# A three-block fp32 transformer kernel: how four norms are summed and awaited on TensorE, and how modulation slabs are scaled

## What is computed

```python
def rms_norm(x, gain):
    y = x * lax.rsqrt(jnp.mean(x * x, axis=-1, keepdims=True) + NORM_EPS)
    return y * gain
def modulate(x, shift, scale):
    return x * (1 + scale[:, None, :]) + shift[:, None, :]
def swiglu(u, w_in, w_out):
    gate, up = jnp.split(u @ w_in, 2, axis=-1)
    return (jax.nn.silu(gate) * up) @ w_out
# first block, for each layer
mod = c_act @ mod_w[layer] + mod_b[layer]
sh1, sc1, g1, sh2, sc2, g2 = jnp.split(mod, N_MOD, axis=-1)
u = modulate(rms_norm(h, norm_mix[layer]), sh1, sc1)
h = h + g1[:, None, :] * mix
u = modulate(rms_norm(h, norm_ffn[layer]), sh2, sc2)
h = h + g2[:, None, :] * swiglu(u, ffn_w_in[layer], ffn_w_out[layer])
# between the layers: shared keys and values from their own norm and modulation
# second block
x = x + rms_norm_2(mixed @ w_out, norm_mix_post)      # the norm "post2"
```

## Time and profile before

| | us |
|---|---|
| median of 3 runs (lowest, highest) | 2295.59 (2285.57, 2300.39) |
| the profiled execution: time | 2293.14 |
| the profiled execution: span, first to last instruction | 2291.3 |
| PE busy | 2157.5 (94% of the span) |
| DVE busy | 1407.9 (61%) |
| ACT busy | 748.5 (33%) |
| POOL busy | 443.2 (19%) |

### The profile page before, as it was taken

How to read it: one execution, slowest core, us unless ns; L and a number is a source line. 1 busy time by engine, 2 the same in 40 slices (tenths; PEclk the granted TensorE clock), 3 DMA queues, 4 the chain that set the end, 5 groups by cost and what they waited for, 6 DMA issues and landing times.

```text
span 2291.3 us, 25604 instructions
## 1 busy us (share of the span) xinstructions
PE 2157.5 (94%) x10020; PEld 1722.6 (75%) x10020; DVE 1407.9 (61%) x1943; ACT 748.5 (33%) x963; POOL 443.2 (19%) x283
## 2 busy tenths in 40 slices
PE   6999999889999989999899999998999998999997
PEld 3787887677888867756678888876568876888885
DVE  7866765556677674377354454477556766655656
ACT  4433243322222223356332222245224234222221
POOL 3000000089988953010000000000410100000000
PEclk9999999999999998999999999999999998999998
DMA  6642321235555543221123222322013221322220
GB/s 216 209 159 93 109 94 56 74 131 208 178 189 178 181 147 129 83 101 56 56 74 109 93 93 94 108 96 68 24 56 111 92 76 72 99 97 99 93 92 37
DMA packets 39371, 248.00 MB, mean 108 GB/s; under 512 B 4927, under 2 KB 5055, under 8 KB 11348
## 3 DMA queue, kind: packets, MB, share of 16 engines
q1 hardware_dynamic: 32820, 228.91, 29.0%
q0 software_dynamic: 3088, 11.16, 1.5%
q10 hardware_dynamic: 3344, 6.29, 0.8%
HBM read 240.05 MB, written 6.29 MB: 108 GB/s over the span
## 4 chain that ended last, share of the span: by engine, by line
PE 82%; DVE 7%; issue 5%; POOL 3%; ACT 2%; DMA 1%; SPq 0%; DVEq 0%; ACTq 0%; POOLq 0%
PE bank L714 24%; PE bank L716 23%; PE bank L715 23%; PE bank L975 2%; DVE w_lo L1934 2%; PE bank L1093 1%; ACT w_hi L1441 1%; PE bank L1103 1%; PE bank L1114 1%; POOL raw L603 1%; DVE scr L1969 1%; PE bank L748 1%; DMA pool<-in_filt_w 1%; PE bank L864 1%; POOL raw L604 1%
## 5 line engine op out<-in xcount | busy, mean ns | idle before, releaser
L714 PE MATMUL bank<-u_hi,w_hi 128*128 128x512 f32 x1708 | 693.7, 406 | 38.7 <-DVE w_lo L1934 11.7
L715 PE MATMUL bank<-u_lo,w_hi 128*128 128x512 f32 x1708 | 671.2, 393 | 0.0
L716 PE MATMUL bank<-u_hi,w_lo 128*128 128x512 f32 x1708 | 671.1, 393 | 0.0
L1934 DVE TENSOR_TENSOR w_lo<-raw,w_hi 128x2048 fp32r<-128x2048 f32 x160 | 424.6, 2654 | 219.6 <-ACT w_hi L1441 219.5
L714 PEld LDWEIGHTS bank<-u_hi,w_hi 128*128 128x128 f32 x1708 | 324.5, 190 | 128.6 <-issue 48.0
L1441 ACT ACTIVATE w_hi<-raw 128x2048 fp32r<-128x2048 f32 x160 | 305.3, 1908 | 346.0 <-PE bank L716 302.9
L716 PEld LDWEIGHTS bank<-u_hi,w_lo 128*128 128x128 f32 x1708 | 324.1, 190 | 69.7
L715 PEld LDWEIGHTS bank<-u_lo,w_hi 128*128 128x128 f32 x1708 | 325.0, 190 | 66.4 <-issue 3.8
L714 PE MATMUL bank<-g_hi,w_hi 128*128 128x512 f32 x772 | 306.6, 397 | 13.4 <-DVE w_lo L1934 6.4
L716 PE MATMUL bank<-g_hi,w_lo 128*128 128x512 f32 x772 | 301.9, 391 | 0.0
L715 PE MATMUL bank<-g_lo,w_hi 128*128 128x512 f32 x772 | 301.9, 391 | 0.0
(11 more groups left out here) (293 smaller groups left out, 2229.9 us busy)
## 6 DMA issues: line engine op xcount, KB each, us to landing
raw<-in_wts SPq DMA_DIRECT2D x216, 1024.0 KB, 4.8
spectra<-pool ACTq DMA_DIRECT2D x16, 256.0 KB, 2.0
scr<-in_rel POOLq DMA_DIRECT2D x16, 256.0 KB, 3.1
pool<-spectra POOLq DMA_DIRECT2D x16, 256.0 KB, 3.1
H<-in_x ACTq DMA_DIRECT2D x1, 2048.0 KB, 24.1
out<-H SPq DMA_DIRECT2D x8, 256.0 KB, 2.0
pool<-in_filt_w POOLq DMA_DIRECT2D x2, 512.0 KB, 12.0
pool<-in_window POOLq DMA_DIRECT2D x1, 1024.0 KB, 17.5
```

The lines of the kernel that those rows point to most:

```text
L714: pe.matmul(out, lh, rh, start=start, stop=False, skip_group_check=True)
L715: pe.matmul(out, lh, rl, start=False, stop=False, skip_group_check=True)
L716: return pe.matmul(out, ll, rh, start=False, stop=stop, skip_group_check=True)
L1934: dve.tensor_tensor(w_lo[RING[w]][:, :], raw[W_STREAM[w] % raw_ring][:, :], w_hi[RING[w]][:, :].bitcast(F32), ALU.subtract).then_inc(lo_do ...
```

## The change

Four things are changed, in the norms "ffn0", "kv", "ffn1" and "post2" and around them.

1. DVE adds only the squares of chunks 0 to 5. PE sums three tiles instead of one (`ssum`, the square of chunk 6 and the square of chunk 7, the last in a buffer of its own, `sq_last`). The add of the sixth square stands behind the last residual. The Sqrt table is loaded ahead of the squares (`root_table`).
2. Between and behind these sums PE repeats a product of two constants, 128x128, into the bank that the next slab will overwrite: 4, 3, 5 and 6 times (`busy`).
3. The slab behind each of these norms, and the first query slab and the gate slab `mgate`, take the two products with `u_hi` as soon as `u_hi` is there, and the product with `u_lo` two chunks later (one later for `mgate` and the first slab of the last stage).
4. The 36 modulation slabs leave the `raw` ring. POOL loads them by its own queue into three buffers `m_buf`, ACT multiplies them by the condition in 8 instructions of 128x256 right behind a weight copy, and POOL keeps the three sums.

```diff
+RING_ITEMS = []
+_m = 0
+for _s in STREAM:
+    _m += _s[0] == "M"
+    if _s[0] == "W" or _m <= M_POOLED:
+        RING_ITEMS.append(_s)
...
+SHORT = ("ffn0", "kv", "ffn1", "post2")
+ADDS = {name: 6 if name in SHORT else KC for name in MAIN}
+ADDED = {name: sum(ADDS[x] for x in MAIN if MAIN[x] < MAIN[name]) for name in MAIN}
...
+        m_buf = [pool[:, a:a + SLOT] for a in (4096, 6144, 12288)]
...
+            def load_mod(m):
+                i = m - M_POOLED
+                pl.dma_start(m_buf[i % 3], A["wts"][M_SOURCE + m]).then_inc(mod_in[i % 3], 16)
...
             def sum_mods():
+                pl.wait_ge(product, READY[FIRST["wo0"]])
+                for m in range(M_POOLED, M_POOLED + 3):
+                    load_mod(m)
                 pl.wait_ge(u_l, U_FFN0 + KC)
                 for m in range(M_POOLED, NM):
...
-                    link(pl.tensor_tensor(chunks, chunks, cact[:, :].unsqueeze(2).broadcast_to((P, KC, 256)), ALU.mult))
+                    pl.wait_ge(m_scaled, KC * (i + 1))
...
+                    if m + 3 < NM:
+                        pl.wait_ge(m_pooled, i + 1)
+                        load_mod(m + 3)
...
-            def norm(name):
+            def norm(name, target=None):
                 n = NORM[name]
...
+                pe.wait_ge(sq_add, ADDED[name] + ADDS[name])
+                pe.wait_ge(*released(n - 1))
+                for x, src in enumerate((ssum, sq[0], sq_last)):
+                    if x:
+                        pe.wait_ge(sq_done, 8 * MAIN[name] + 6 + x)
+                    for j in range(TB):
+                        mm = pe.matmul(bank[6][:, j:j + 1], src[:, j * P:(j + 1) * P], onec[:, :], start=(x == 0 and j == 0),
+                                       stop=(x == 2 and j == TB - 1), skip_group_check=True)
+                    if target is not None and x < 2:
+                        busy(target, (4, 3)[x])
+                mm.then_inc(n_col, 1)
+                if target is not None:
+                    busy(target, 5)
                 norm_bc(n)
+                if target is not None:
+                    busy(target, 6)
+
+            def busy(n, count):
+                b = claim(n)
+                for _ in range(count):
+                    pe.matmul(b[:, 0:P], ident[:, :], ones[:, :], start=True, stop=True)
+
+            def slot_lag(label, i, first, count, lag, nout=2):
+                w, hi, lo = weights(label, i)
+                banks = [claim(first + j) for j in range(nout)]
+                for k in range(KC + lag):
+                    if k < KC:
+                        pe.wait_ge(u_h, count + k + 1)
+                        for j in range(nout):
+                            c = k * 256 + j * P
+                            pe.matmul(banks[j][:, :], hi[:, c:c + P], u_hi[:, k, :], start=(k == 0), stop=False, skip_group_check=True)
+                            pe.matmul(banks[j][:, :], lo[:, c:c + P], u_hi[:, k, :], start=False, stop=False, skip_group_check=True)
+                    if k >= lag:
+                        x = k - lag
+                        wait_u(count + x + 1)
...
-            norm("post2")
-            lead = mlp_slot(0)
+            norm("post2", FIRST["mi0"])
+            lead = mlp_lead()
             follow = mlp_slot(1)
-            for k in range(KC):
+            for k in range(KC + 1):
                 next(lead)
                 if k >= 2:
                     next(follow)
...
+            def scale_mod(m):
+                i = m - M_POOLED
+                act.wait_ge(mod_in[i % 3], 16 * (i // 3 + 1))
+                for k in range(KC):
+                    x = m_buf[i % 3][:, k * 256:(k + 1) * 256]
+                    act.activation(x, x, ACT.Identity, bias=zcol[:, 0:1], scale=cact[:, k:k + 1]).then_inc(m_scaled, 1)
...
                     act.activation(w_hi[RING[w]][:, :], raw[s % raw_ring][:, :], ACT.Copy).then_inc(hi_done, 1)
+                    for m in range(M_POOLED, NM):
+                        if M_BEFORE[m] == w:
+                            scale_mod(m)
...
-            ffn("0", G_FFN0, 0, G2_0, "wo0", lambda c: add_square("kv", c))
-
-            add_square("kv", KC - 1)
+            ffn("0", G_FFN0, 0, G2_0, "wo0", lambda c: c < ADDS["kv"] and add_square("kv", c))
```

More of the change, by code:

```diff
@@ L453, in build @@
         rel_ready, mask_ready, taps_in = sem("rel_ready"), sem("mask_ready"), sem("taps_in")
+        m_scaled = sem("m_scaled")
+        mod_in = [sem(f"mod_in{x}") for x in range(3)]
         w4_in, row_done, row_out = sem("w4_in"), sem("row_done"), sem("row_out")
@@ L560, in _ @@
             w = m = 0
[L561 removed]
+            for s, item in enumerate(RING_ITEMS):
                 if s >= raw_ring:
@@ L1116, in weighted @@
                 mm.then_inc(at_v, 1)
-            for step in query_steps(0):
-                pass
+            slot_lag("qq", 0, FIRST["qq"], U_MIX1, 2)
             pe.wait_ge(mod_col, NVMOD)
@@ L1151, in _ @@
                 pass
-            norm("ffn1")
+            norm("ffn1", FIRST["fi1_0"])
             ffn("1", U_FFN1, G_FFN1)
@@ L1624, in _ @@
                 ahead("wo0", i)
+                if i == 0:
+                    root_table("ffn0")
                 squares("ffn0", H, (2 * i, 2 * i + 1))
```

100 lines of the change are left out of this document (68 added, 32 removed).

## The result

| kernel | median of runs, us | ratio to before, 95% interval |
|---|---|---|
| before | 2294.35 (7 runs, 2285.57 to 2301.25) | |
| changed | 2280.63 (7 runs, 2276.60 to 2283.89) | 0.9937 [0.9917, 0.9958] |

The changed kernel is 0.6% faster, 14.5 us by the ratio; 2281 us had been predicted. The profiled execution took 2281.22 us, with a span of 2279.4 us. The total was right and its terms were not: the modulation slabs gave far more than was put down for them, and the norms cost time where they were to win some.

The account below looks back on a forecast made before the run. PE, busy 94% of the span, bounds the kernel, with waits and half-clock products at norms. Terms -0.5 - 6.3 + 1.3 + 4.5 - 1.6 - 10 = -12.6 us gave 2280.5 profiled, 2281 us forecast; range 2263 to 2299.

Parts of the forecast that it names:

- The modulation slabs: First feed-forward stage: waits for split slabs and residuals (7.6 and 4.7 us) mostly vanish; -10 us, between 0 and -13.
- a return of the waits: First feed-forward stage: PE's waits might come back from ACT, whose scaling was put at 3.3 us per slab; gain then 0.
- a sum of -5 us: Whole kernel: if three splits on PE's path wait for POOL's sums, the slabs give -2 and the total is -5.
- ffn0: Norm "ffn0": second slab 2.9 us sooner if the clock holds, 1.8 us later if it falls; -0.5 us taken.
- kv: Norm "kv": collision of POOL with DVE's add goes, sums start earlier; -6.3 us, middle of -8.7 and -3.9.
- ffn1: Norm "ffn1": second slab 1.1 us sooner with the clock held or 3.7 us later with it fallen; +1.3 us taken.
- The prediction's own sign: Norms: the forecast fails if they gain more than 20 us or lose in sum, or if PE comes to wait for ACT.
- post2: Norm "post2": later root moves DVE's queue and the pair ends later, so the output slab starts 3.2 to 5.8 later; +4.5 us.
- First query slab: First query slab: starts some 0.9 us sooner on `u_hi`, may spare a clock fall; -1.6 us, between -2.6 and 0.
- The clock falls in all four: Rival, four norms: 18 extra products run at half speed, norms win nothing; -3.6 us, 2290 us, chance 0.22.
- The clock holds: Rival, four norms: constant products bridge them and keep full clock; -25.1 us, 2268 us, chance 0.24.
- The loads come late: Rival, modulation loads on POOL's queue: landing beyond about 22 us slows the kernel; some +25 us, 2318 us, chance 0.08.

Follow-up runs that it names:

- e1: Kernel before with only the modulation slabs changed: out of the ring, ACT scaling, POOL summing; norms and slab order untouched. 2269.15 us, ratio 0.9892.
- e5: Kernel before with the modulation slabs out of the ring, in buffers on POOL's queue, but POOL keeping its product. 2296.38 us, ratio 1.0016.
- e9: Changed kernel with its constant products moved from between the sums to ahead of the wait for them, more behind the broadcast. 2267.45 us, ratio 0.9889.
- e10: e8 with fifteen constant products ahead of the sums at "kv" and the same filling in "post2". 2258.18 us, ratio 0.9852.
- e2: Changed kernel with the modulation slabs back in the ring, so norms, lagged slabs and constant products alone. 2303.42 us, ratio 1.0035.
- e3: Changed kernel without its constant products in the four norms (`busy` never called). 2271.82 us, ratio 0.9903.
- e7: e1 with lagged first slabs (feed-forward, key, query), without the new norms and constant products. 2266.98 us, ratio 0.9894.
- e8: e7 with constant products where PE waits in ffn0, kv, ffn1: ahead of the sums, behind them, behind the broadcast. 2260.22 us, ratio 0.9861.

## Why the prediction was right, and where it was wrong

**The modulation slabs: mis-sized.** The term was -10 us, at most -13. e1 shows -24.8, and by its stages 18.8 us fell in the first feed-forward stage and 5.9 at "kv" (109.0 to 103.1), which had been booked under that norm. The step that failed is the one that took the gain from PE's listed waits, 12.3 us, put nearly nothing on top of them and then took off for a return of the waits. The listed waits were right: PE's idle time in that stage fell by 12.5 us in e1. On top came fewer products at half clock. One less the granted clock, times PE's busy time, added up over windows of 1 us, is 6.2 us before and 3.0 in e1, which is an estimate; 1.8 of the 6.2 lie behind the 6.82 us wait (the granted clock was 0.52 from 485 to 490 and 0.79 to 495, PE busy 1.58 and 5.00 us, so 1.58 x 0.48 + 5.00 x 0.21). The last 3 us or so are stalls too small for the list. The column sums of the modulations mark each slab: in the changed kernel they come every 11.35 us; before, nine of the 28 intervals from 513.75 us on are 0.3 to 2.3 us longer.

In the kernel before:

```profile
689.46 0.51 PE L748 MATMUL bank<-onec,macc 128*128 128x1 f32 x4
...
701.42 0.51 PE L748 MATMUL bank<-onec,macc 128*128 128x1 f32 x4
...
712.77 0.51 PE L748 MATMUL bank<-onec,macc 128*128 128x1 f32 x4
```

In the changed kernel:

```profile
693.66 0.51 PE L771 MATMUL bank<-onec,macc 128*128 128x1 f32 x4
...
705.02 0.51 PE L771 MATMUL bank<-onec,macc 128*128 128x1 f32 x4
```

From 513.75 to 839.13 the kernel before took 325.4 us for 28 slabs, the changed one 317.9 (512.01 to 829.90): 7.5 us, where the list had 4.7 in its waits for `H`. The rule that a split meeting one of POOL's sums still waits for the whole of it, which the Trainium skill's page *SBUF — State Buffer* (section "Who interferes with whom") gives, would have left a sum of -5 us by my reckoning. e5 agrees with the rule (splits of 4.01 us on average, with POOL hardly ever idle). In the changed kernel the meetings hardly happen: at "kv" ACT's 4.03 us of scaling start with DVE's split, and POOL waits for them, so its sum at 870.38 begins after the split's end at 868.68. The mean of 2.31 us says that nearly all splits went free. The term also took ACT's scaling at 8 x 0.416 = 3.3 us; it took 4.0, and hid all the same.

**"ffn0", "kv", "ffn1": the fallen clock, not the middle.** I took the middle between a clock that holds and one that falls. It fell in all four during the sums or the products between them (broadcasts of 1.91, 1.91, 1.42 and 1.76 us, where 1.12 is full clock). Counted from the last product ahead of the norm, the forecast for the first scaling and the second slab, and what was measured:

| us | scaling, held or fallen | measured | second slab, held or fallen | measured |
|---|---|---|---|---|
| ffn0 | 8.2 or 12.9 | 11.95 | 21.8 or 26.5 | 25.57 |
| kv | 8.4 or 13.2 | 13.10 | 22.0 or 26.8 | 26.72 |
| ffn1 | 8.2 or 13.0 | 11.29 | 21.8 or 26.6 | 24.91 |

The mechanism was right, the three sums, the products at half speed and the second slab 13.6 us behind the scaling; the choice between its two sizes was not. That the clock was low behind 32 one-column instructions was read, and weighed too little; a rule it is not, as the clock held through 24 of them in two norms of e9. What I had not seen is that the products need not stand between the sums: e10, with one sum per norm and products only where PE waits, holds the clock in all four norms.

The prediction's own sign, that it fails if the norms lose in sum, came true: the four stages of e2 are 10.0 us longer than before.

**"kv": right, for the other edit's sake.** The collision with POOL went as described (the first sum waits 1.51 us). But it goes with the modulation slabs, not with the norm: e1 has that gain without the new norm, and e2 has the norm without the gain.

**"post2": right.** +4.5 [+3.2, +5.8] was forecast, 42.1 us against 37.2 and 38.4 is +3.7 to +4.9. The reason holds as well: DVE's split begins behind the root (1895.74, then 1897.84), and PE's wait ahead of the output slab grew from 2.13 to 3.91 us. e3 shares the loss out: with no constant products 39.1 us are left, so 3 of the 4 to 5 us are theirs.

**First query slab: larger, and for another reason.** -1.6 was forecast, the stage fell by 5.7 us (means 180.1 and 174.4). But e1, with the old order there, is at 175.6. PE's idle time in this stage is 10.6 us in the traces of before and in e1, and 10.1 in those of the changed kernel, so the lag took away 0.5 us of it. The rest is clock. In both traces of before it fell three times in this stage: behind the 2.17 us wait for `u_lo`, behind a 2.50 us wait for DVE in the attention, and some 150 us on. With the same old order it fell once in e1 and twice in e5, not behind the 2.17 us wait in either; in the two traces of the changed kernel it fell never and once. e7 against e1, in this stage the new order alone, is 175.2 against 175.6 us. So no more than half a microsecond is shown to be the lag's.

**The rivals.** "The clock falls in all four" was right about the norms (its four terms add up to +7.4 us, the four stages of e2 to +10.0) and wrong about the total, since it kept -10 for the slabs. "The clock holds" did not come about in this kernel; e10 shows that it can in all four norms, with the old sums. "The loads come late" fell: POOL's 36 loads landed 5.2 us after issue in the median, against the 22 from which it decides. The Trainium skill's *DMA: Bandwidth & Descriptors* (section "Anatomy of one DMA") gave 4.4 by my estimate, and the trace bears that out within 0.8 us.

So the total came out by luck, from two errors that cancel: norms and query -2.6 forecast and +8.0 measured alone, slabs -10 forecast and -24.8 measured alone.

## What to carry to other kernels

An engine with slack can still set the pace of another that works beside it. Where such a partner is, the stretched durations of the other engine's instructions show; what its removal is worth is the bottleneck's listed waits, here 12 us, and the products at half clock behind them, here some 3 us, and stalls too small for the list. Half of the edit may be worth nothing. Work that is there only to keep TensorE's clock belongs where TensorE waits anyway; on the chain that ends the wait it cost more here than the clock gave back (2280.63 us against 2271.82 without). Before a stage's difference between two traces is put down to an edit, look at how that stage differs between two traces of one kernel.

## What the runs showed of the hardware that was not expected

The granted clock behind the same idle time of PE fell in one execution and not in another. Behind 3.27 or 3.28 us in the head the next product took 0.76 or 0.77 us in seven of the thirteen traces and 0.47 in six; at the gate slab, behind 2.33 to 2.35 us, the clock fell in three of thirteen. The head, with the same products of PE, took 445 to 452 us in these traces.

A wait of 1.33 us with products ahead of it was followed by a fall (e8 at "kv"), one of 0.58 us in the same kernel was not.

POOL's own sums gain from the parting too: its first sum took 3.47 us and takes 2.40 when no split of DVE runs beside it.
